# Layer 0's pair gathers: where PE's side work, the spreads of h and two key steps stand between the up products

## The chip, the cores and the metric

The kernel runs on one core of a Trainium2 chip. The metric is the device time of one execution in microseconds (us). Engines are named as in the profile: PE is TensorE (PEld its weight loads), DVE VectorE, ACT ScalarE, POOL GpSimd, SP SyncE.

## What is computed

Two transformer-like blocks in float32 over 256 tokens of width 1024. The first has two layers; each mixes tokens (latent attention, a Fourier branch, a pooling branch, gates) and then runs `_peer`, a lookup of experts. Layer 0 does this for two streams, x and ctx, layer 1's lookup for x alone. The lookup, cut to what matters here:

```
q = (h @ w_pq).reshape(B, L, PEER_HEADS, 2, PEER_QDIM // 2)
s = jnp.einsum("blhpd,hpkd->blhpk", q, peer_keys)
sv, si = lax.top_k(s, PEER_TOPK)                  # 16 of 128 keys, twice per head
...                                               # 16 of the 256 pairs of keys: eidx, gate
a = jnp.einsum("tkd,td->tk", peer_down[eidx], h)  # 8 heads x 16 = 128 experts a token
act = gate * gelu(a)
out = jnp.einsum("tk,tkd->td", act, peer_up[eidx])
```

The second block (feed-forward, convolution, attention over blocks) comes after and is not touched.

## The kernel before, in words

**Gathers.** A row of `peer0` holds an expert's down and up vector, 8 KB. For one stream and one tile of 128 tokens, 128 gathers bring 128 rows each (1 MB). In layer 0 a gather is spread: it brings 4 experts for each of the 32 tokens of one quarter of the tile. There are 4 x 128 = 512 such gathers, in the order x0 tile 0, x0 tile 1, c0 tile 0, c0 tile 1 (x0 and c0 are the two streams in layer 0, x1 and c1 in layer 1). `SPREADS` (line 102) lists for each its index column, its quarter and its set. A set is a group of heads whose routing ends together: heads 0, 1, 2 to 3, 4 to 7 for the first tile and 0 to 3, 4 to 7 for the second. Within a set, all gathers of quarter 0 come first, then those of quarter 1, and so on.

**What one gather n passes through.** POOL issues it (L2825) into one of six places; it waits for up product n-6, that is for its place to be free. DVE multiplies the 128 down vectors with h and sums (`spread_down`, L2347, the "down product", 1.22 us); h lies in PSUM, spread so that each quarter of the partitions holds the 32 tokens of the current quarter. ACT makes the weights in six instructions, the last L1815 (`spread_diag`). PE multiplies them with the up vectors and sums them in PSUM (`spread_up`, L1240, the "up product", four records a gather). Its end lets POOL issue gather n+6. When the quarter changes (`new_quarter`, line 105), PE must spread h anew (`spread_h`, L1227, 16 records), after the last down product of the old quarter and before the first of the new one. There are 48 such spreads.

**Half groups and side work.** `gather` on each engine handles four gathers (`HALF`) and then, or in between, a list of other stages, the side work: query products and scores (`pq`), top-k routing (`route`, on DVE), sending indices to their quarters (`moved`, PE's L1189 and ACT's L1766), gates (`gpre`, `gate`), Fourier steps, attention, output projection, keys and values. `beside_x0` and `beside_c0` say by hand which stages stand in which of the 128 half groups; `scoring` lists those that run before the first gather of a stream, `begin` those of the first half groups.

DVE and ACT do all four down products, or all four weights, and then the side stages. All queues are in order, so weights n+4 stand behind ACT's part of the side stages of half group n, and down product n+4 behind DVE's.

PE does the side stages of half group n first. Inside long products `between()` (called before each matmul, a "piece" below) runs an up product after every fourth piece, up to up n+2. After the stages come what is left of these, then `spread_h(n+4)` if due, then up n+3:

```
last_up[0] = n + HALF - 1
run_stages(stages)
ups_to(n + HALF - 1)
last_up[0] = 0
if n + HALF < len(SPREADS) and new_quarter(n + HALF):
    spread_h(n + HALF)
ups_to(n + HALF)
```

A stage without `between()` (transposes, broadcasts, `moved`) lets no up product through. A query step `pq` has 16 pieces for the queries and 4 for the scores of the block before. SP loads the weight blocks of the side work (`wring`, 1 MB) when the product that used the slot has ended; beside the gathers two slots are in use.

**Places that the change names.** `scoring("x0")` ends with query block 2 and then the routing and sending of the first head; `begin` puts blocks 3 and 4 into half group 0 of x0. `beside_c0` puts layer 1's key steps 0 and 1 (norm of the keys; their transposes) into half group 364, step 2 into 368, step 3 into 372.

Of the kernel before, what the change touches and what calls it, by code (L numbers as in the profile page):

```python
# [13 lines left out]
P = 128  # L14
# [14 lines left out]
TOP = 16  # L29
# [3 lines left out]
HALF = GROUP // 2  # L33
# [20 lines left out]
QUADS = P // QUAD  # L54


def keys_stages(r):
    return [("scale", r, 0), ("norm", r, 0), ("hT", r, 0), ("zA", r, 0), ("zA", r, 1)] + [("kv", r, k) for k in range(4)]
# [8 lines left out]
def branches(r):  # L67

    return [[("zF", r, 0)], [("zF", r, 1)], [("four", r, 0), ("q", r, 0)], [("four", r, 1), ("q", r, 1)], [("q", r, 2)], [("q", r, 3)]]
# [11 lines left out]
def routes(r, t, ks):  # L81

    return [st for k in ks for st in [("route", r, t, k, 0), ("route", r, t, k, 1)] + [("moved", r, t, k)] * (k >= 8 and r != "x1")]


SETS = [[(0, 1), (1, 2), (2, 4), (4, 8)], [(0, 4), (4, 8)]]
# [9 lines left out]

def spread_gathers(t):

    return [(TOP * h0 + QUADS * s + j, j, n) for n, (h0, h1) in enumerate(SETS[t]) for j in range(QUADS) for s in range(TOP * (h1 - h0) // QUADS)]


SPREADS = [g for _ in range(2) for t in range(TT) for g in spread_gathers(t)]


def new_quarter(n):
    return n % P == 0 or SPREADS[n][1:] != SPREADS[n - 1][1:]


def scoring(r):

    first = routes(r, 0, (0, 8))
    return [[("take", r)], [("pq", r, 0)], [("pq", r, 1)], first[0:4], [("pq", r, 2)], first[4:]]


def spread(slots, ranks, counts):

    for n, take in counts:
        while take:
            slots[n].append(ranks[0])
            take -= ranks[0][0] == "route"  # L120
            ranks = ranks[1:]
        if ranks and ranks[0][0] == "moved":
            slots[n + 1].append(ranks[0])
            ranks = ranks[1:]
    assert not ranks


def one_each(n0, count, at):

    where = [at(n0, n) for n in range(count)]  # L130
    return [(n, where.count(n)) for n in sorted(set(where))]


def begin(r, slots):

    slots[0] += [("pq", r, 3)] + [("pq", r, 4)] * (r == "x0") + routes(r, 0, (1,))
    slots[1] += [("pq", r, 5 if r == "x0" else 4)] + routes(r, 0, (9,))[0:2]
    slots[2] += routes(r, 0, (9,))[2:]
    for n, c in ((2, 6), (3, 7), (4, 8)) if r == "x0" else ((3, 5), (5, 6), (7, 7), (9, 8)):
        slots[n].append(("pq", r, c))  # L140
    ranks = routes(r, 0, RANKS[0][4:])
    spread(slots, ranks, ((2, 1), (3, 1), (4, 2), (5, 2), (6, 2), (7, 1), (8, 1), (9, 1), (10, 1), (11, 1), (12, 2), (13, 1)))
# [49 lines left out]
def beside_c0(late):  # L192

    slots = [[] for _ in range(2 * TT * GROUPS)]

    def place(n, st, step=1):
        for i, s in enumerate(st):
            slots[n + i * step].extend(s if isinstance(s, list) else [s])

    at = -1  # L200
    for st in late:
        at += st[0] == "route"
        slots[at + (st[0] == "moved")].append(st)
    at += 1
    spread(slots, routes("c0", 1, RANKS[1]), one_each(at, 20, lambda a, n: a + n - (n + 1) // 5))
    at += 16
    k = keys_stages("x1")
    slots[2].append(k[0])
    slots[4].append(k[1])
    place(5, k[2:5] + [("gpre", "x1", dp, j) for dp in range(3) for j in (1, 2)], 2)  # L210
    assert at < 30
    place(at, [k[5:7]] + k[7:])
    zf0, zf1, one, two, *last = branches("x1")
    place(32, [zf0, [one[1]] + zf1, [one[0]], [two[0]]] + last + [("gpre", "x1", dp, 0) for dp in range(3)], 2)
    slots[39].append(two[1])
    place(50, [("ybc", "x1", 0), ("ybc", "x1", 1), ("gpre", "x1", 3, 1), ("gpre", "x1", 3, 2), ("ybc", "x1", 3), ("ybc", "x1", 2), ("gpre", "x1", 3, 0)], 2)
    slots[40].append(("scale", "c1", 0))
    slots[44].append(("norm", "c1", 0, 0))
    slots[63].append(("hT", "c1", 0, 0))
    return slots  # L220
# [248 lines left out]
def chunk_slots(count):  # L469

    wide, middle, slots, last, used = first_chunks(), middle_chunks(), [], {}, {}
    narrow = narrow_chunks()
    for n in range(count):
        s = n % (SLOTS + ROW_SLOTS) if n < wide else min(range(SLOTS + ROW_SLOTS if n in middle else SLOTS - 1 if n < narrow else SLOTS), key=lambda m: last[m])
        slots.append((s, used.get(s, 0), last.get(s)))
        last[s], used[s] = n, used.get(s, 0) + 1
    return slots


def build(nc, A, out):  # L480
# [19 lines left out]
    with ctx:  # L500
# [46 lines left out]
        at = [0]  # L547
# [155 lines left out]
        slots = chunk_slots(len(plan))  # L703
# [19 lines left out]
        def taken(eng, run, banks):  # L723

            for b in banks:
                eng.wait_ge(bank_free[b], taken_at[run if run == "x1" else "x0", b])
# [6 lines left out]
        def h_mark(run, k, n):  # L733

            firsts = {"c0": 0, "x0": 1, "x1": 4}
            return (firsts[run] if k == 0 else {"x0": 2, "c0": 3, "x1": 5}[run]) * 2 + n
# [19 lines left out]
        def spread_place(n):  # L756

            k = n % SPREAD_PLACES
            return both[k] if k < HALF else lent[n > LENT] if k == HALF else wring[:, SLOTS - 1, :]
# [5 lines left out]
        def _(pe):  # L765
# [42 lines left out]
            next_up, last_up, pieces = [0], [0], [0]  # L808
# [6 lines left out]

            def ups_to(n):
                while next_up[0] < n:
                    spread_up(next_up[0])
                    next_up[0] += 1
                    pieces[0] = 0  # L820
# [393 lines left out]
            def spread_h(n):  # L1214

                run, t = GATHERS[n // P]
                j = SPREADS[n][1]
                pe.wait_ge(mark["h"], h_mark(run, 1, 2))
                if n == 0:
                    taken(pe, run, TAKEN)  # L1220
                else:
                    pe.wait_ge(down_done, n)
                one_of = ident[:, QUAD * j:QUAD * (j + 1)]
                for half in range(2):
                    for i in range(QUADS):
                        qd = QUAD * i
                        ins = pe.matmul(h_ps[qd:qd + QUAD, half * 512:(half + 1) * 512], one_of, h[RUNS[run][0]][:, t, half * 512:(half + 1) * 512],  # L1227
                                        start=True, stop=True, tile_position=(0, qd), skip_group_check=True)
                ins.then_inc(h_spread, 1)

            def spread_up(n):

                t, j = n // P % TT, SPREADS[n][1]
                mine = [k for k in range(n // P * P, n // P * P + P) if SPREADS[k][1] == j]
                if n % P == 0:
                    pe.wait_ge(sum_read, n // P)
                pe.wait_ge(diag_ready, n + 1)
                for half in range(2):
                    qd = QUAD * ((j + 2 * half) % QUADS)
                    ins = pe.matmul(ps[qd:qd + QUAD, UPB + half, :], quad_w[:, n % GROUP, :], spread_place(n)[:, D + half * 512:D + (half + 1) * 512],  # L1240
                                    start=(n == mine[0]), stop=(n == mine[-1]), tile_position=(0, qd), skip_group_check=True)
                ins.then_inc(upp_done, 1)

            def gather(run, t, n0, beside_a, beside_b):

                G = GATHER_NO[run, t]
                for part_, stages in enumerate((beside_a, beside_b)):
                    if run == "x1":
                        i = PAIRS * t + 2 * (2 * n0 + part_)
                        run_stages(stages)  # L1250
                        if i:
                            both_ups(i - 1)
                        both_ups(i)
                        if i == 2 * PAIRS - 2:
                            both_ups(i + 1)
                        continue
                    n = P * G + HALF * (2 * n0 + part_)
                    if n == 0:
                        spread_h(0)
                    last_up[0] = n + HALF - 1  # L1260
                    run_stages(stages)
                    ups_to(n + HALF - 1)
                    last_up[0] = 0
                    if n + HALF < len(SPREADS) and new_quarter(n + HALF):
                        spread_h(n + HALF)
                    ups_to(n + HALF)

            def fb(run, t):
# [1684 lines left out]
```

## Time and profile before

| | us |
|---|---|
| three timed runs | 3846.46, 3848.91, 3853.41 |
| their median | 3848.91 |
| the profiled execution | 3838.83 |
| its span | 3837.0 |
| busy in it: PE, DVE, ACT, POOL | 3174.7, 2396.1, 1605.2, 743.1 |
| DMA traffic | 1158 MB, mean 302 GB/s |

The profiled execution is one run with the hardware profiler; its span goes from its first to its last instruction. All rows below are from it, with times in us from the span's start. Busy times of engines overlap. Layer 0's gathers lie between 367 and 1925 us, layer 1's behind that, then the second block.

### The profile page before, as it was taken

What the parts mean: (1) busy time and instruction counts of PE and PEld (TensorE: products, weight loads), DVE (VectorE), ACT (ScalarE), POOL (GpSimd) and SP (SyncE); (2) the same over time, 40 slices, a digit from 0 to 9 for tenths busy, and PEclk for the clock granted to TensorE, in tenths of its full rate; (3) what the DMA queues carried; (4) which work ended last, traced back from release to release, by engine and by line L of the source; (5) the groups of instructions that cost most, each with busy time, mean ns of one, the idle gap of its engine ahead of it and who ended that gap; (6) DMA issues with size and microseconds to landing.
All of it is one profiled execution on the core that took longest, in us unless ns stands there. A gap on an engine that the chain in (4) does not pass through costs nothing.

```text
span 3837.0 us, 44307 instructions
## 1 busy us (share of the span) xinstructions
PE 3174.7 (83%) x15370; PEld 1938.4 (51%) x15370; DVE 2396.1 (62%) x5191; ACT 1605.2 (42%) x4579; POOL 743.1 (19%) x797
## 2 busy tenths in 40 slices
PE   5898977888896875767778877777799989999899
PEld 2485533233351231122346432333397879898798
DVE  3444678555568777454455887786665866565564
ACT  1432455565555555655542111112233533334433
POOL 0000233233323323333301333333200000000000
PEclk8998998899897887888989989999999989999999
DMA  7665999999999998999925999999754235454454
GB/s 292 271 252 212 343 396 393 356 393 407 409 393 379 388 368 347 407 402 413 418 96 225 396 402 420 401 413 415 295 186 171 93 121 195 165 197 170 142 175 154
DMA packets 163870, 1158.01 MB, mean 302 GB/s; under 512 B 18785, under 2 KB 19553, under 8 KB 26978
## 3 DMA queue, kind: packets, MB, share of 16 engines
q0 software_dynamic: 110592, 805.36, 51.7%
q1 hardware_dynamic: 53090, 350.30, 25.0%
q8 instruction: 99, 1.62, 0.2%
q14 instruction: 89, 0.73, 0.1%
HBM read 1154.53 MB, written 1.05 MB: 301 GB/s over the span
## 4 chain that ended last, share of the span: by engine, by line
PE 54%; DVE 18%; DMA 17%; ACT 6%; issue 4%; POOL 0%; SPq 0%; DVEq 0%; POOLq 0%; ACTq 0%
PE ps L1304 9%; PE ps L1302 9%; PE ps L1303 9%; PE ps L1240 7%; DMA rows<-in_peer,diag 5%; PE ps L1210 4%; DMA h_ctx<-in_peer,idx 3%; PE ps L1159 3%; DMA rows<-in_peer,idx 3%; DMA wring<-in_peer,diag 3%; PE ps L1105 3%; PE ps L903 2%; DVE rows L2347 2%; PE ps L1131 2%; DVE shared L2557 1%
## 5 line engine op out<-in xcount | busy, mean ns | idle before, releaser
L2347 DVE CUSTOM_DVE_ANT_0 rows<-rows,ps 128x1024 f32<-128x1024 f32 x342 | 408.8, 1219 | 304.2 <-DMA rows<-in_peer,diag 228.6
L1240 PE MATMUL ps<-rows,diag 128*32 128x512 f32 x1368 | 413.7, 700 | 178.6 <-ACT diag L1815 175.8
L2825 POOL DMA_INDIRECT rows<-in_peer,diag x342 | 324.2, 948 | 1075.9 <-PE ps L1240 698.1
L1302 PE MATMUL ps<-hT_hi,w_hi 128*128 128x256 f32 x1792 | 508.0, 283 | 8.9 <-DVE hT_lo L2469 8.9
L1304 PE MATMUL ps<-hT_lo,w_hi 128*128 128x256 f32 x1792 | 508.7, 284 | 0.0
L1303 PE MATMUL ps<-hT_hi,w_lo 128*128 128x256 f32 x1792 | 506.9, 283 | 0.0
L1302 PEld LDWEIGHTS ps<-hT_hi,w_hi 128*128 128x128 f32 x1792 | 343.3, 192 | 14.4 <-issue 14.3
L2459 DVE TENSOR_TENSOR w_lo<-wring,w_hi 128x2048 fp32r<-128x2048 f32 x120 | 274.8, 2292 | 112.0 <-ACT w_hi L1874 110.2
L1303 PEld LDWEIGHTS ps<-hT_hi,w_lo 128*128 128x128 f32 x1792 | 342.6, 191 | 0.1
L1304 PEld LDWEIGHTS ps<-hT_lo,w_hi 128*128 128x128 f32 x1792 | 341.5, 191 | 0.0
L1210 PE MATMUL ps<-rows,diag 128*128 128x512 f32 x512 | 252.3, 644 | 80.2 <-ACT diag L1799 73.2
L1806 ACT ACTIVATE g<-a 128x1 f32<-128x1 f32 x512 | 99.7, 195 | 444.4 <-DVE a L2347 443.8
L1240 PEld LDWEIGHTS ps<-rows,diag 128*32 128x32 f32 x1368 | 61.2, 117 | 430.0 <-ACT diag L1815 350.9
L1874 ACT ACTIVATE w_hi<-wring 128x2048 fp32r<-128x2048 f32 x120 | 229.3, 1911 | 112.9 <-DMA wring<-in_wdn 83.6
L1210 PE MATMUL ps<-kvmem,diag 128*128 128x512 f32 x384 | 192.4, 648 | 63.1 <-ACT diag L1799 63.1
L1793 ACT ACTIVATE th<-g 128x2 f32<-128x2 f32 x128 | 26.1, 204 | 488.5 <-DVE g L2326 488.5
L2849 POOL TENSOR_TENSOR ss<-nwt,minus_half 128x1 f32<-128x1 f32 x24 | 13.2, 548 | 1083.4 <-DVE nwt L2031 1083.4
L1210 PEld LDWEIGHTS ps<-rows,diag 128*128 128x128 f32 x512 | 101.2, 205 | 226.1 <-issue 113.6
L1813 ACT ACTIVATE act<-th,gated 128x1 f32<-128x1 f32 x512 | 198.2, 387 | 17.2
L1105 PE MATMUL ps<-hT,wring 128*128 128x256 f32 x768 | 198.6, 403 | 0.1
L2836 POOL DMA_INDIRECT rows<-in_peer,idx x128 | 121.5, 950 | 397.1 <-PE ps L1210 232.4
L2321 DVE CUSTOM_DVE_ANT_0 rows<-rows,ps 128x1024 f32<-128x1024 f32 x128 | 153.7, 1218 | 62.2 <-DMA rows<-in_peer,idx 58.8
(355 smaller groups left out, 6226.2 us busy)
## 6 DMA issues: line engine op xcount, KB each, us to landing
wring<-in_wgu SPq DMA_DIRECT2D x66, 1024.0 KB, 4.9
wring<-in_wdn SPq DMA_DIRECT2D x33, 1024.0 KB, 4.9
wring<-in_wG SPq DMA_DIRECT2D x32, 1024.0 KB, 8.2
wring<-in_wmod SPq DMA_DIRECT2D x28, 1024.0 KB, 7.9
wring<-in_wpq SPq DMA_DIRECT2D x24, 1024.0 KB, 7.2
rows<-in_wgu SPq DMA_DIRECT2D x22, 1024.0 KB, 4.9
rows<-in_wmod SPq DMA_DIRECT2D x20, 1024.0 KB, 7.7
rows<-in_wdn SPq DMA_DIRECT2D x11, 1024.0 KB, 4.8
```

The costliest lines, as they stand in the source:

```text
L1105: last = pe.matmul(b[:, dt * TOK:(dt + 1) * TOK], w[:, k * 256 + dt * P:k * 256 + (dt + 1) * P], hT[:, k, :], start=(k == 0), stop=(k == K ...
L1210: ins = pe.matmul(ps[:, UPB + half, :], diag[:, s, :], both[s][:, D + half * 512:D + (half + 1) * 512], start=(first and j == 0), stop=(la ...
L1240: ins = pe.matmul(ps[qd:qd + QUAD, UPB + half, :], quad_w[:, n % GROUP, :], spread_place(n)[:, D + half * 512:D + (half + 1) * 512], start ...
L1302: pe.matmul(out_, lh[l_at], rh[r_at], start=start, stop=False, skip_group_check=skip)
L1303: pe.matmul(out_, ll[l_at], rh[r_at], start=False, stop=False, skip_group_check=skip)
L1304: return pe.matmul(out_, lh[l_at], rl[r_at], start=False, stop=stop, skip_group_check=skip)
L1813: act.activation(act_, th, ACT.Identity, scale=weight, bias=weight).then_inc(gelu_step, 1)
L1874: act.activation(W2_HI[c % SLOTS2], W2[c % SLOTS2], ACT.Copy).then_inc(hi_ready, 1)
L2321: dve.tensor_tensor_reduce(out=both[c][:, 0:D], in0=both[c][:, 0:D], in1=h_ps, scale=1.0, scalar=0.0, op0=ALU.mult, op1=ALU.add, accum_out ...
L2347: dve.tensor_tensor_reduce(out=down, in0=down, in1=h_ps, scale=1.0, scalar=0.0, op0=ALU.mult, op1=ALU.add, accum_out=a8[:, c:c + 1]).then_ ...
L2459: dve.tensor_tensor(W2_LO[c % SLOTS2], w, W2_HI[c % SLOTS2].bitcast(f32), ALU.subtract).then_inc(lo_ready, 1)
L2825: pool.indirect_dma_start(out=spread_place(n), out_offset=None, in_=A["peer0"], in_offset=bass.IndirectOffsetOnAxis(ap=idx_moved[t][:, col ...
```

## The change

1. The order of quarters in every second set is reversed (0 to 3, then 3 to 0), and `new_quarter` no longer counts a change of set with the same quarter: 40 spreads of h for 48. The eight that fall away are ahead of gathers 16, 32, 64, 192, 272, 288, 320 and 448.
2. In `gather` on PE, up n comes before the side stages of half group n, and `between()` may run all ups up to n+3. `ups_to` itself spreads h for the next half group when it is about to run up n+3.
3. For x0, query block 3 runs before the sending of the first set's indices and so before the first gather; half group 0 keeps block 4.
4. Layer 1's key steps 0, 1, 2 and 3 stand in half groups 364, 368, 372 and 376.

```
 def spread_gathers(t):
-    return [(TOP * h0 + QUADS * s + j, j, n) for n, (h0, h1) in enumerate(SETS[t]) for j in range(QUADS) for s in range(TOP * (h1 - h0) // QUADS)]
+    to_and_fro = range(QUADS), range(QUADS - 1, -1, -1)
+    return [(TOP * h0 + QUADS * s + j, j, n) for n, (h0, h1) in enumerate(SETS[t]) for j in to_and_fro[n % 2] for s in range(TOP * (h1 - h0) // QUADS)]

 def new_quarter(n):
-    return n % P == 0 or SPREADS[n][1:] != SPREADS[n - 1][1:]
+    return n % P == 0 or SPREADS[n][1] != SPREADS[n - 1][1]

 def scoring(r):
     first = routes(r, 0, (0, 8))
-    return [[("take", r)], [("pq", r, 0)], [("pq", r, 1)], first[0:4], [("pq", r, 2)], first[4:]]
+    return [[("take", r)], [("pq", r, 0)], [("pq", r, 1)], first[0:4], [("pq", r, 2)]] + [[("pq", r, 3)], first[4:]] * (r == "x0")

 def begin(r, slots):
-    slots[0] += [("pq", r, 3)] + [("pq", r, 4)] * (r == "x0") + routes(r, 0, (1,))
+    slots[0] += [("pq", r, 4 if r == "x0" else 3)] + routes(r, 0, (1,))

 in beside_c0:
-    place(at, [k[5:7]] + k[7:])
+    place(at, k[5:])

             def ups_to(n):
                 while next_up[0] < n:
+                    k = next_up[0] + 1
+                    if k % HALF == 0 and k < len(SPREADS) and new_quarter(k):
+                        spread_h(k)
                     spread_up(next_up[0])
                     next_up[0] += 1
                     pieces[0] = 0

 in gather on PE:
                     if n == 0:
                         spread_h(0)
-                    last_up[0] = n + HALF - 1
+                    ups_to(n + 1)
+                    last_up[0] = n + HALF
                     run_stages(stages)
-                    ups_to(n + HALF - 1)
                     last_up[0] = 0
-                    if n + HALF < len(SPREADS) and new_quarter(n + HALF):
-                        spread_h(n + HALF)
                     ups_to(n + HALF)
```

## Rows read from the trace of the kernel before

**Rows 1.** The page, DMA engines' busy share in 40 equal slices, in tenths.
```profile
DMA  7665999999999998999925999999754235454454
```
**Rows 2.** Windows: length, busy time (instructions) by engine, PE's clock, DMA share, GB/s.
```profile
367.40:1925.00 1557.60, 1206.87 (x5008) 475.21 (x5006) 963.16 (x2234) 870.98 (x3319) 485.66 (x512) 0.89 0.96 387
...
1505.00:1521.00 16.00, 5.14 (x29) 1.31 (x24) 8.36 (x36) 7.48 (x31) 1.31 (x2) 0.50 0.10 29
```
**Rows 3.** Windows: first query blocks, context's gates and outputs, its queries, half group 216.
```profile
402.80:448.10 45.30, 42.44 (x233) 23.88 (x234) 24.35 (x68) 21.92 (x83) 11.39 (x12) 1.00 0.96 347
892.20:997.60 105.40, 97.60 (x351) 40.86 (x350) 57.64 (x94) 49.87 (x196) 30.62 (x32) 0.98 1.00 409
1035.30:1141.10 105.80, 102.67 (x490) 58.88 (x490) 56.86 (x142) 56.83 (x213) 29.98 (x32) 1.00 1.00 410
1060.42:1072.93 12.51, 12.51 (x57) 7.38 (x56) 4.92 (x8) 7.06 (x28) 4.68 (x5) 1.00 1.01 412
```
**Rows 4.** The page's costliest groups: up products, with PE's idle time before them.
```profile
L1240 PE MATMUL ps<-rows,diag 128*32 128x512 f32 x1368 | 413.7, 700 | 178.6 <-ACT diag L1815 175.8
```
**Rows 5.** Timeline (start, length, engine, line, operation), from half group 216 to 220.
```profile
1069.47 1.05 PE L1170 MATMUL ps<-keysT,shared 128*128 128x128 f32 x8
...
1070.46 1.05 PE L1240 MATMUL ps<-rows,diag 128*32 128x512 f32 x4
...
1070.57 0.60 ACT L1561 ACTIVATE shared<-ps 128x512 f32<-128x512 f32 x1 [0.29 <-PE ps L1170]
...
1071.44 1.56 PE L1159 MATMUL ps<-hT,wring 128*128 128x256 f32 x6
...
1072.40 0.32 ACT L1815 ACTIVATE diag<-quad,act 128x32 f32<-128x32 f32 x1
```
**Rows 6.** Timeline, a gate's last products and the next weights (176 to 180).
```profile
943.74 0.81 PE L1131 MATMUL ps<-ypT,wring 128*128 128x256 f32 x3
...
948.62 0.32 ACT L1815 ACTIVATE diag<-quad,act 128x32 f32<-128x32 f32 x1
```
**Rows 7.** Line L2825 (gathers) from 1035 to 1141: POOL's waits, time to landing.
```profile
  PE ps L1240: 71.5, 30
...
DMA to landing us min/median/max: 5.7/8.5/11.0
```
**Rows 8.** Line L2825 from 892 to 997: time to landing.
```profile
DMA to landing us min/median/max: 6.5/10.6/14.1
```
**Rows 9.** Timeline of PE, layer 1's first transposes and the ups behind them.
```profile
1240.07 3.67 PE L883 MATMUL ps<-ident,h_in 128*128 128x128 f32 x16 [5.99 <-DVE h_in L2123]
1244.71 3.49 PE L1240 MATMUL ps<-rows,diag 128*32 128x512 f32 x8 [0.97 <-ACT diag L1815]
```
**Rows 10.** Line L2347 (down products): DVE's idle time before it until a spread's end.
```profile
  PE ps L1227: 69.7, 17
```
**Rows 11.** Timeline of PE in half group 0 of x0, up to up 4.
```profile
376.43 1.92 PE L1240 MATMUL ps<-rows,diag 128*32 128x512 f32 x4 [8.82 <-ACT diag L1815]
...
389.85 7.07 PE L1159 MATMUL ps<-hT,wring 128*128 128x256 f32 x32
...
397.74 1.92 PE L1227 MATMUL ps<-h_in,ident 128*32 128x512 f32 x16
...
402.82 1.05 PE L1240 MATMUL ps<-x_ctx,diag 128*32 128x512 f32 x4 [0.81 <-ACT diag L1815]
```
**Rows 12.** Timelines of ACT, PE, POOL and DVE at the hole near 1505.
```profile
1507.09 0.32 ACT L1815 ACTIVATE diag<-quad,act 128x32 f32<-128x32 f32 x1
...
1516.13 0.66 PE L939 MATMUL ps<-ident,shared 128*128 128x128 f32 x2 [10.86 <-DVE shared L2148]
1516.71 1.92 PE L1240 MATMUL ps<-kvmem,diag 128*32 128x512 f32 x4
...
1518.92 0.94 POOL L2825 DMA_INDIRECT kvmem<-in_peer,diag  x1 [20.49 <-PE ps L1240]
...
1523.40 1.22 DVE L2347 CUSTOM_DVE_ANT_0 rows<-rows,ps 128x1024 f32<-128x1024 f32 x1 [5.29 <-PE ps L1227]
```
**Rows 13.** Timeline of PE, an up product after a wait.
```profile
1253.94 1.14 PE L1240 MATMUL ps<-kvmem,diag 128*32 128x512 f32 x4 [2.30 <-ACT diag L1815]
```

## The prediction

> **What bounds the kernel now.** I read the page first, for what the DMA engines do in each slice: nine tenths or more in nearly all of slices 5 to 19 (the first is slice 0), and full again in later ones [rows 1]. The change touches layer 0's 512 pair gathers alone. The first is issued at 367.4, the last up product ends at about 1925; over these 1557.6 us the DMA share is 0.96 [rows 2]. So all idle DMA time there is 0.04 x 1557.6 = 62 us, and a change of order can save no more. The longest hole is 1505 to 1521, with a share of 0.10, which is 14.4 us idle [rows 2]. Outside the holes the DMA engines are full, but in places only just. While context's query products run beside the gathers (below: half groups 208 to 236; I name a half group by its first gather) PE is busy 102.67 of 105.8 us at a DMA share of 1.00; for context's gates and outputs (164 to 192) it is 97.60 of 105.4 us, also at 1.00 [rows 3]. There either engine alone can lengthen the stretch. PE's own wait before the up products is for ACT's weights, 175.8 of 178.6 us on the rows buffers [rows 4].
>
> The loop of one half group is what the change rearranges. From up 216 to up 220 it took 12.51 us, PE busy 12.51 of them [rows 3]. Four rows and one weight block of 1 MB (2^20 bytes each) are 5.24 MB, at 412 GB/s [rows 3] 12.7 us. PE and DMA are level.
>
> **Part 1: the first up product ahead of the side work, the last one inside it.** The same instructions are issued. In the old order PE runs three pieces, up n, four, up n+1, four, up n+2, the rest, the spread of h if one is due, up n+3. In the new one: up n, three pieces, up n+1, four, up n+2, four, spread, up n+3, the rest. Then it stands at the wait for up n+4. ACT works in order: its copy of the side product stands ahead of the weights of gather n+4, and can start only when PE's last piece ends. PE's products end at 1069.47 + 1.05 = 1070.52, ACT's copy starts at 1070.57, the weights are there at 1072.40 + 0.32 = 1072.72 [rows 5]: a tail of 2.25 us from last piece to next up. Today up n+3 (1.05) and three pieces (1.56) cover it [rows 5]. Afterwards both stand elsewhere, and nothing covers it.
> - Context's queries, eight half groups. They take 105.8 us [rows 3], which is 8 x 12.5, two spreads of 1.92 and 2 us of waits. After: 8 x (12.5 + 2.25) + 3.8 = 121.8. **+16** (8 if queueing in front of the DMA takes half of it; 20 at most).
> - Context's gates and outputs, eight. Here the tail goes through DVE's mixing, the down product and ACT: a gate's products end at 943.74 + 0.81 = 944.55, the weights are ready at 948.62 + 0.32 = 948.94 [rows 6], 4.4 us. Six of the eight end so (an output's first part is not evacuated). PE's work is 4 ups of 1.0 and products of 7.6, so after: 8 x 11.6 + 1.9 + 6 x 4.4 = 121.1, today 105.4 [rows 3], 16 more. Transfers take 10.6 us from issue to landing here, where the least in the query stretch is 5.7 [rows 7, 8]: up to 4.9 us of lateness may come out of this queueing. **+12** (5 to 17).
> - Attention steps with a gate product (128, 136, 144): a tail of 2.3 or more each, partly absorbed. **+4** (0 to 7).
> - Transposes. The first transposes of context's second norm and of layer 1 (204 and 276) have no places for ups. Today they run in the wait ahead of up n: 3.67 us from 1240.07, then up 276 at 1244.71 and its neighbour right behind [rows 9]. Afterwards they stand between up n and up n+1, so gather n+7 goes out 3.67 later, in a hole, where nothing is queued. **+7** (3 to 7.4).
> - The Fourier and query steps (104 to 120), the norm at 432 and the last transposes at 508 have the same form with more slack: **+5** (0 to 10), by the nearest rows, those of the tail and of the transposes.
> - Gate products in every other half group (from 300 on): the pair needs about 20 us of PE and 22.7 of DMA, so the tail fits: 0.
>
> **Part 2: h spread within the side work, and 40 spreads for 48.** DVE waited 69.7 us in 17 places for a spread [rows 10], 4 each. A spread takes PE 1.92 us [rows 11]. Of the eight that fall away one (row 16) is where PE is the bound; it is counted in part 3. DVE's next down product starts earlier, but its weights stand behind ACT's copy, so this helps only where DVE itself is the bound. Together with up n moved ahead of the index products ("moved") it shortens the other holes, 62 - 14.4 = 48 us in sum, by a little, and later ups pay in some: **-3** (-10 to 0).
>
> **Part 3: x0's query block 3 before the first gather.** The index products of the first set now stand behind 16 + 4 pieces, 7.07 + 1.05 us [rows 5, 11], so the first gather goes out 8.1 later, at 375.5. SP's next weight block goes out when that product ends, about 372 for 389, into an idle DMA; POOL's queue only shifts. In return half group 0 holds 20 pieces for 40. Up 0 at 376.43 + 8.1 = 384.5 [rows 11]; up 1 after 1.9 and four pieces at the lower clock (3.2, estimated as twice today's), up 2 after 2.9, up 3 after 1.0 + 1.9 + 1.9 with the spread, so 397.3; 1.0 + 3.3 to the end of the products, 2.25 of tail: up 4 at 403.9, today 402.82 [rows 11]. Half groups 4 and 8 take 12.5 + 1.9 + 2.25 = 16.65 where they now take 45.3 / 3 = 15.1 [rows 3]; 12, without a spread, 14.75. By row 16 PE is 4 us late, but DVE, which sets the pace from there on and gets its h early, is 1 us early. **+1** (-2 to +4).
>
> **Part 4: layer 1's key steps apart.** Up 364 stands behind the transposes of the normed keys, for which PE waited 10.86 us; its weights were there at 1507.41, it ran at 1516.71, and POOL issued the next gather at 1518.92, after 20.49 us [rows 12]. In the new order up 364 runs at 1507.5 and gather 370 goes out at about 1509, three more by 1514. h for 368 is spread at 1511, so its down product can run when DVE has ended the norm, 1516.1, and not at 1523.40 [rows 12]. What is late next is DVE's routing, which ends at 1504.5, and this norm. Of 14.4 idle us some 5.5 stay: **-9** (-12 to -7).
>
> **Sum.** 16 + 12 + 4 + 7 + 5 - 3 + 1 - 9 = +33 us. The profiled execution took 3838.8 us (span 3837.0), 10 below the median of the timed runs, 3848.9. I add the difference to the median: **3882 us**. Behind 1925 nothing changes; that work waits for the last up product.
>
> **Rivals.**
> - *Queueing swallows the tails* (faster). Place: the joints of half groups 164 to 236. Gathers take 8.5 and 10.6 us to land there, 5.7 at the least [rows 7, 8]. The ups of a group now come early within it; if that keeps rows queued over the tail, only the DMA's 12.7 us per half group count. Then keys (-9), holes (-8) and transposes (+5) are left: -12, 3837. It decides from the point where PE's work and tail fall under 12.7; I get 14.75. Against it: of POOL's waits in the query stretch 71.5 us were for PE [rows 7]. 0.13.
> - *Nothing measurable.* Half of part 1's terms (22) less 12 to 20 from holes and keys: about +2 to +10, taken as 3852. 0.12.
> - *PE's clock falls at the joints* (slower still). After 8.82 us of waiting an up took 1.92 us, at the higher clock 1.05 [rows 11]. The granted clock was 1.00 in the query stretch and 0.50 in the hole at 1505 [rows 2, 3], that is 2.4 and 1.2 GHz. If it fell at half of 20 joints, each would cost 0.87 for the up and 1.5 for three pieces at half the rate: 10 x 2.3 = 23 on top, 3905. 0.12. Against it: after a wait of 2.30 us an up still took 1.14 [rows 13]. The Trainium skill, "TensorE: Matmul & The Clock Gate", section "Loop structure matters more than you think", says that a long wait between bursts lets the clock drop and the next matmul runs cold; by that rule the joints of the gates would be in danger first, and the 1.92 us above agree with it.
>
> **Numbers.** The forecast has 0.63. Faster by over 0.2% (7.7 us, about what a measurement of this kernel can tell from no change) 0.13; within it 0.12; slower 0.63 + 0.12 = 0.75. The bounds of the terms add up to -8 and +58; 3845 to 3908 leaves out the first rival and a little at the top.
>
> **What would show it.** PE's L1240 should wait some 2.3 us for ACT once in each half group from 208 to 236, and up 208 to up 240 should take about 122 us at a DMA share near 0.87. The transposes should follow up 276. The hole near 1505 should shrink to 4 to 6 us and POOL's wait of 20.49 to about 11. The first gather should come at 375.5. I am wrong if the query stretch keeps its 106 us (then the first rival holds), and wrong upwards if ups of 1.92 us fill it.

## The result, and the profile after

The changed kernel takes 3950.42 us (median of 4 runs, 3946.37 to 3958.28), the kernel before 3847.68 beside it: a ratio of 1.0268, 95% interval 1.0246 to 1.029. It is 102.7 us slower. The forecast was 3882, range 3845 to 3908: the sign was right, the size a third of what came. A *joint* below is the place where one half group ends and the next begins, the *tail* the time there from PE's last piece to its next up product.

The page of the changed kernel: PE's granted clock and the DMA engines' share in 40 slices, and the up products' group (busy, mean ns of one, idle time before it).

```profile
PEclk8998998888888888888888999999999989999999
DMA  7766899888888999899962899999955325454444
L1244 PE MATMUL ps<-rows,diag 128*32 128x512 f32 x1368 | 416.7, 703 | 283.1 <-ACT diag L1817 276.0
```

Beside [rows 1], slices 7 to 12 have fallen from nine tenths or more to eight. Beside [rows 4] the same 1368 up products stand behind 283.1 us of idle time, 276.0 of it for ACT's weights, instead of 178.6. The span is 3955.7 us for 3837.0; the profiled execution of the changed kernel is 8 us above its median and that of the kernel before 9 below, so the stretches read here differ by some 16 us more in sum than the medians. The last up product starts at 2039.1 for 1923.8, so 115 of the 119 us more lie ahead of it, in the pair gathers, as the prediction said; behind it little moved.

Windows of the changed kernel from up product to up product (columns as in [rows 2]): up 0 to 20, 20 to 124, 124 to 164 (attention), 164 to 196 (gates, outputs), 208 to 240 (context's queries), 364 to the last.

```profile
381.30:462.20 80.90, 67.28 (x330) 35.77 (x330) 47.44 (x138) 35.70 (x134) 18.87 (x20) 0.94 0.90 338
462.20:797.50 335.30, 251.37 (x1028) 102.40 (x1028) 233.19 (x603) 176.51 (x680) 100.64 (x104) 0.89 0.94 367
797.50:927.00 129.50, 100.33 (x406) 42.23 (x407) 62.97 (x125) 77.38 (x292) 37.56 (x40) 0.87 0.88 345
927.00:1062.90 135.90, 111.35 (x342) 45.14 (x344) 57.88 (x95) 49.70 (x196) 30.10 (x32) 0.87 0.84 323
1101.80:1234.50 132.70, 113.54 (x488) 63.31 (x488) 59.80 (x150) 56.46 (x213) 30.00 (x32) 0.92 0.88 326
1606.90:2039.10 432.20, 313.03 (x1147) 106.24 (x1147) 202.80 (x379) 245.44 (x940) 133.16 (x142) 0.85 0.94 378
```

Three of these between the same ups in the kernel before; the other two are in [rows 3].

```profile
459.40:780.00 320.60, 251.50 (x1050) 98.68 (x1052) 233.00 (x604) 178.11 (x684) 99.57 (x104) 0.90 0.96 383
780.00:892.20 112.20, 92.04 (x408) 38.82 (x407) 62.01 (x123) 75.99 (x289) 37.46 (x40) 0.95 0.98 396
...
1516.70:1923.80 407.10, 307.05 (x1145) 102.24 (x1144) 198.67 (x357) 241.66 (x916) 133.30 (x142) 0.87 0.98 402
```

Read the length minus PE's busy time as PE's idle time, and the two rises apart:

| half groups | before | after | more | PE idle | PE busy |
|---|---|---|---|---|---|
| 20 to 120 | 320.6 | 335.3 | 14.7 | +14.8 | -0.1 |
| 124 to 160 | 112.2 | 129.5 | 17.3 | +9.0 | +8.3 |
| 164 to 192 | 105.4 | 135.9 | 30.5 | +16.8 | +13.8 |
| 208 to 236 | 105.8 | 132.7 | 26.9 | +16.0 | +10.9 |
| 364 to 508 | 407.1 | 432.2 | 25.1 | +19.1 | +6.0 |

The instructions are the same (but for two spreads of h fewer in 20 to 120, and one in 164 to 192 and in 364 to 508; the counts differ by a few more since some records are missing), so a rise of PE's busy time means that it runs slower: the clock column went from 0.95 to 0.87 in attention, from 0.98 to 0.87 in gates and outputs, from 1.00 to 0.92 in the queries. In the queries, the cleanest stretch, PE's idle time rose by the forecast 16 us; the busy part was no term of the sum at all.

One joint of the query stretch in the changed kernel (timeline: start, length, engine, line, operation):

```profile
1144.68 1.05 PE L1174 MATMUL ps<-keysT,shared 128*128 128x128 f32 x8
...
1145.77 0.60 ACT L1563 ACTIVATE shared<-ps 128x512 f32<-128x512 f32 x1 [0.29 <-PE ps L1174]
...
1147.61 0.32 ACT L1817 ACTIVATE diag<-quad,act 128x32 f32<-128x32 f32 x1
...
1147.98 1.05 PE L1244 MATMUL ps<-kvmem,diag 128*32 128x512 f32 x4 [2.25 <-ACT diag L1817]
1148.96 2.68 PE L1163 MATMUL ps<-hT,wring 128*128 128x256 f32 x6
1151.58 1.57 PE L1244 MATMUL ps<-wring,diag 128*32 128x512 f32 x4
1153.08 1.99 PE L1163 MATMUL ps<-hT,wring 128*128 128x256 f32 x8
```

ACT's copy of the last score product, its weights for gather 220, and PE bare for 2.25 us in between: the tail of the prediction, with its length. What follows was not in the prediction's sum. The up product behind the wait still takes 1.05 us, but the next three pieces take 2.68 us where [rows 5] has 1.56, and the next up 1.57; the pieces behind that run as before. At six of the eight joints of the stretch the first up product takes 1.05 us like this one, at 224 and 228 it takes 1.83 and 1.35, behind waits of 2.25 and 2.35 us. PE's waits in that stretch and in gates and outputs, and the up product behind one of the gates:

```profile
PE ps L1244 <- ACT diag L1817: 18.3, 8, 2.5
```
```profile
PE ps L1244 <- ACT diag L1817: 26.0, 7, 4.5
```
```profile
962.38 1.92 PE L1244 MATMUL ps<-kvmem,diag 128*32 128x512 f32 x4 [4.45 <-ACT diag L1817]
```

Here, behind 4.45 us, the up itself runs at the lower rate.

The other parts. The hole of part 4, with the transposes now behind the up (PE, then POOL):

```profile
1606.95 1.07 PE L1244 MATMUL ps<-kvmem,diag 128*32 128x512 f32 x2 [10.79 <-ACT diag L1817]
...
1609.15 0.94 POOL L2827 DMA_INDIRECT kvmem<-in_peer,diag  x1 [11.22 <-PE ps L1244]
```

POOL waits 11.22 us where [rows 12] has 20.49 (forecast about 11). The up stands 10.79 us itself, now for its own weights behind DVE's norm. The hole in the transfers has shrunk as forecast: 15 x 0.34 = 5.1 us idle for 14.4.

```profile
1597.00:1612.00 15.00, 5.05 (x40) 2.22 (x42) 11.27 (x19) 6.32 (x26) 2.80 (x3) 0.66 0.66 261
```

Layer 1's first transposes follow up 276, as forecast:

```profile
1337.22 1.92 PE L1244 MATMUL ps<-rows,diag 128*32 128x512 f32 x4 [8.78 <-ACT diag L1817]
1339.07 2.59 PE L887 MATMUL ps<-ident,h_in 128*128 128x128 f32 x16
```

The first gather is issued at 372.11, 4.7 us later than before, not 8.1.

### The profile page after: what moved, and what is told of

Same layout as the page of the kernel before. It is cut to its first block, busy times and chain, and to the rows that moved or that the text cites. A ratio compares the mean times of both kernels' runs of the same rounds, so it can differ in the third digit from the quotient of the medians.

```text
span 3955.7 us, 44041 instructions
## 1 busy us (share of the span) xinstructions
PE 3202.7 (81%) x15242; PEld 1952.5 (49%) x15242; DVE 2394.6 (61%) x5191; ACT 1600.9 (40%) x4579; POOL 742.7 (19%) x797
## 3 DMA queue, kind: packets, MB, share of 16 engines
HBM read 1154.53 MB, written 1.05 MB: 292 GB/s over the span
## 4 chain that ended last, share of the span: by engine, by line
PE 57%; DVE 16%; DMA 15%; ACT 8%; issue 3%; POOL 0%; SPq 0%; DVEq 0%; ACTq 0%; POOLq 0%
PE ps L1304 9%; PE ps L1306 9%; PE ps L1305 9%; PE ps L1244 8%; PE ps L1214 4%; DMA rows<-in_peer,diag 4%; PE ps L1163 4%; PE ps L1109 4%; DMA h_ctx<-in_peer,idx 3%; DMA rows<-in_peer,idx 3%; PE ps L907 2%; PE ps L1135 2%; DVE rows L2349 2%; DMA kvmem<-in_peer,diag 2%; ACT act L1815 1%
## 5 line engine op out<-in xcount | busy, mean ns | idle before, releaser
L1244 PE MATMUL ps<-rows,diag 128*32 128x512 f32 x1368 | 416.7, 703 | 283.1 <-ACT diag L1817 276.0
L2349 DVE CUSTOM_DVE_ANT_0 rows<-rows,ps 128x1024 f32<-128x1024 f32 x342 | 408.6, 1219 | 359.7 <-DMA rows<-in_peer,diag 278.1
L1304 PEld LDWEIGHTS ps<-hT_hi,w_hi 128*128 128x128 f32 x1792 | 343.9, 192 | 14.4 <-issue 14.3
L1244 PEld LDWEIGHTS ps<-rows,diag 128*32 128x32 f32 x1368 | 60.3, 117 | 532.5 <-ACT diag L1817 437.0
L1109 PEld LDWEIGHTS ps<-hT,wring 128*128 128x128 f32 x768 | 145.8, 200 | 99.9 <-issue 82.4
```

Of the source, the lines that this page charges most:

```text
L1109: last = pe.matmul(b[:, dt * TOK:(dt + 1) * TOK], w[:, k * 256 + dt * P:k * 256 + (dt + 1) * P], hT[:, k, :], start=(k == 0), stop=(k == K ...
L1304: pe.matmul(out_, lh[l_at], rh[r_at], start=start, stop=False, skip_group_check=skip)
L2349: dve.tensor_tensor_reduce(out=down, in0=down, in1=h_ps, scale=1.0, scalar=0.0, op0=ALU.mult, op1=ALU.add, accum_out=a8[:, c:c + 1]).then_ ...
```

## The experiments

In what follows a stretch is named by its ups. The parts are numbered as in the prediction: *part 1* is the order on PE (first up product ahead, last one inside), *part 2* the order of the quarters. The spread of h inside the side work, which the prediction counts to part 2, comes and goes with part 1 in every run.

**The changed kernel without part 1.**

```
-                    k = next_up[0] + 1
-                    if k % HALF == 0 and k < len(SPREADS) and new_quarter(k):
-                        spread_h(k)
 in gather on PE: the lines of before
```

> The changed kernel with PE's loop of before for a half group (side work, the last up product behind it, h spread at the end): parts 2, 3 and 4 stay, part 1 is gone. Theory A (the whole loss is the joint of two half groups, where PE stands before the first up product: 184.5 us before, 366.1 us after): 3848 - 9 (keys) - 3 (quarters) + 1 (query block) = 3837, within 3828 to 3846. Theory B (a good part of the loss comes from the later first gather, the quarters to and fro or the key steps): over 3860.

Measured: 3839.61 us, ratio 0.9972 (0.9961 to 0.9983): faster than the kernel before. Its query stretch:

```profile
1038.40:1144.20 105.80, 102.67 (x490) 58.74 (x492) 56.92 (x142) 56.83 (x213) 29.98 (x32) 1.00 1.01 410
```

It is that of [rows 3] to the hundredth in PE's busy time. So part 1 (with its spreads of h) costs 3950.4 - 3839.6 = 111 us, and parts 2 to 4 together give about 9. Theory B falls.

**Which half of part 1?** First the last up product, and the spread of h in front of it, put behind the side work again:

```
-                    last_up[0] = n + HALF
+                    last_up[0] = n + HALF - 1
```

> The changed kernel, but the last up product of a half group, and the spread of h in front of it, stand behind the side work again; the first stays ahead. Theory A: the last piece's tail (piece, ACT's copy, ACT's weights) is then covered by 1.05 us of up product, and by 1.92 more where h is spread; at some 45 joints with side work that is 45 x 1.05 + 15 x 1 = 62 off, 3888 (3870 to 3910). Theory B (the harm is in the first up product ahead, not in the bare tail): 3940 or more. Theory C (the harm is the last up product inside the side work): 3855 or less.

Measured: 3916.33, ratio 1.017 (1.015 to 1.0191). 34 of the 111 us come back, less than theory A's 62 and 6 us outside its range; theories B and C do not fit either. In the query stretch theory A holds:

```profile
1078.10:1193.60 115.50, 102.10 (x490) 59.84 (x492) 56.80 (x142) 56.87 (x213) 29.97 (x32) 1.00 0.97 373
```

With the up product of 1.05 us over the tail, 8 x (2.25 - 1.05) = 9.6 on top of 105.8 are due, and 9.7 show. The clock is 1.00 again: most joints of this stretch now wait 1.27 us, and PE's busy time is back at 102.10. Elsewhere cover of one up was worth less than I had summed; why is not shown.

**Side work ahead again, the last up product still inside.**

```
-                    ups_to(n + 1)
                     last_up[0] = n + HALF
```

> The changed kernel, but the side work begins ahead of the first up product again, as before; the last up product and the spread of h stay within the side work. Theory A: at the joint the next half group's first three pieces (1.56 us with query products) cover the tail of 2.25 us but for 0.7, so the context's queries (half groups 208 to 236) lose 8 x 0.7 = 6 us at most and the whole stands at 3837 + 6 = 3843 (3832 to 3860). Theory C (last up product inside the side work does the harm, since nothing stands behind the last piece): 3900 or more.

Measured: 3894.52, ratio 1.0123 (1.0106 to 1.014). That is far outside theory A's range and near theory C, and the query stretch even took what the changed kernel's does. Its window, and the joint near 1106 on PE's timeline:

```profile
1062.20:1195.60 133.40, 113.50 (x482) 63.91 (x483) 59.89 (x148) 56.66 (x213) 29.98 (x32) 0.91 0.88 328
```
```profile
1105.13 1.05 PE L1174 MATMUL ps<-keysT,shared 128*128 128x128 f32 x8
1108.52 1.05 PE L1244 MATMUL ps<-kvmem,diag 128*32 128x512 f32 x4 [2.34 <-ACT diag L1816]
```

No piece stands between the last score product and the first up. `between()` counts pieces since the last up product. Where that one is inside, the pieces behind it are counted into the next half group; with four score products behind it, the next up is due at once. The edit had not put the side work first where it mattered.

**The same with the count cleared.**

```
-                    ups_to(n + 1)
+                    pieces[0] = 0
                     last_up[0] = n + HALF
```

> The changed kernel with the side work ahead of the first up product and the last one within it, as the run before, but with the count of pieces set to 0 at the start of each half group. Theory A': in that run the count was carried over from the pieces behind the last up product (four score products in the context's query steps), so the first up product was due at once and stood bare at the joint although the code put the side work ahead; its query stretch took 133.4 us, as the changed kernel's 132.7. With the count at 0, three pieces of 0.39 us or more lead and cover all but 0.7 of the 2.25: the query stretch takes 106 to 112 us and the whole 3840 to 3860. Theory C (a last up product inside the side work is bad by itself): the query stretch stays near 133 and the whole at 3890 or more.

Measured: 3864.52, ratio 1.0039 (1.0027 to 1.0051), 4.5 us above the expected band. The query stretch:

```profile
1054.70:1167.30 112.60, 103.41 (x490) 57.88 (x492) 58.58 (x146) 56.64 (x212) 30.03 (x32) 1.00 0.98 385
```
```profile
PE ps L1244 <- ACT diag L1817: 8.9, 9, 1.6
```

Three pieces cover the tail but for 0.95 us at most joints, and 133.4 us become 112.6, at the upper end of what A' has; C falls. The rest above the kernel before lies there (7 us), in attention (7) and in the gates (up 164 to 180 takes 68.2 us, 57.8 before), where the tail of 4.4 us is longer than three pieces.

**The clock by itself.** PE is kept busy at the joints from 124 to 240 by products of zero weights (8 a joint, 16 behind gates and outputs), which leave the accumulator as it is. The added product, without the loop around it:

```
+                        pe.matmul(ps[qd:qd + QUAD, UPB, 0:P], ident[0:QUAD, QUAD:2 * QUAD], ident[0:QUAD, :],
+                              start=False, stop=False, tile_position=(0, qd), skip_group_check=True)
                     ups_to(n + 1)
```

> The changed kernel with PE kept busy while it waits at the joints of half groups 124 to 240: 8 products of zero weights (32 x 32 by 128 columns, 16 behind gates and outputs) added into the up product's own accumulator, which they leave as it is. They lie in a wait of 2.25 us or more. Theory A with the clock (after a wait PE's products run at the lower clock: PE's busy time in those stretches rose by 8.3, 4.7, 9.0 and 10.9 us): up to 33 us come back, 3917 to 3935. Theory D (the lower clock costs nothing, since the wait for rows sets the pace): 3945 to 3955. If the products outlast the wait, they push the time up, past 3955.

Measured: 3950.3, ratio 1.0269 (1.0249 to 1.0289): nothing gained in sum, as theory D has it. By stretch it is two things, up 180 to 196 (16 products a joint) and the queries (8):

```profile
999.90:1068.70 68.80, 68.80 (x260) 28.85 (x260) 24.64 (x41) 25.67 (x101) 15.12 (x16) 0.90 0.77 284
1106.50:1229.40 122.90, 118.62 (x616) 71.95 (x616) 60.05 (x150) 56.47 (x212) 29.99 (x32) 1.00 0.93 353
```

The first was 60.9 us in the changed kernel and now has no idle time at all: at two of its four joints (184 and 192) there was no wait to fill, at the others 3.38 us, and the filling takes 3.7 at each. The second fell by 9.8, at a clock of 1.00. So it was tried with the query stretch alone.

> The changed kernel with PE kept busy in the wait at the joints 212 to 240 alone, by 8 products of zero weights each. In the run that did it from 124 to 240 the query stretch fell from 132.7 to 122.9 us at a granted clock of 1.00 for 0.92, but 16 products per joint outlasted the waits behind the outputs (60.9 to 68.8 us), so the whole stood still. Theory A with the clock: 8 joints x 1.36 = 10.9, of which 9.8 show: 3940 (3935 to 3945). Theory D (no gain from the clock; the 9.8 were a shift between stretches): 3950.

Measured: 3944.24, ratio 1.024 (1.0225 to 1.0255). The query stretch, and its groups on PE (busy, mean ns of one, idle before); behind it the pieces of the same stretch in the changed kernel:

```profile
1102.60:1227.10 124.50, 120.20 (x616) 72.50 (x616) 60.08 (x150) 56.48 (x213) 29.98 (x32) 0.99 0.93 348
```
```profile
L1163 PE MATMUL ps<-hT,wring 128*128 128x256 f32 x256 | 64.5, 395 | 0.0
...
L1252 PE MATMUL ps<-ident 32*32 32x128 f32 x128 | 15.4, 269 | 0.0
```
```profile
L1163 PE MATMUL ps<-hT,wring 128*128 128x256 f32 x256 | 70.8, 424 | 0.0
```

The stretch became 8.2 us shorter, and the pieces alone take 6.3 us less. The filling is 15.4 / 8 = 1.9 us a joint, inside the 2.25. The median of the whole fell by 6.2, within the range, but the intervals of the two kernels touch (1.0225 to 1.0255, 1.0246 to 1.029), so the whole by itself doesn't show it. The stretch does, in two runs: work added in a wait made it shorter, so the clock is a cost of its own here, and about a microsecond a joint of it came back.

**Is it the queue on ACT and DVE?** PE's order stays the changed one; the next half group's first down product and weights go ahead of the side work on DVE and ACT, where no new spread is due (so 128 keeps the old order too, beside the six that the expectation lists).

```
+def early(n):
+    return int(124 < n < 244 and not new_quarter(n))

 in gather on ACT and on DVE:
-                        for k in range(n, n + HALF):
+                        for k in range(n + early(n), n + HALF + early(n + HALF)):
```

> The changed kernel; DVE's down product and ACT's weights of the next half group's first gather stand ahead of this half group's side work on their engines, from half group 124 to 240, wherever that gather needs no new spread of h (22 of 29 joints; 144, 160, 176, 208, 224 and 240 keep the old order). PE's order is untouched. Theory A (the bare tail, and it is one of queue order: ACT's copy or DVE's mixing in front of the weights): the freed joints lose tail and lower clock, 6 x (2.25 + 1.4) = 22 in the query stretch (132.7 to 111), 26 of 30 in gates and outputs, 12 of 17 in attention: 3890 (3880 to 3910). Rival (the rows themselves come too late, the joint waits for the transfer whatever stands in ACT's queue): the shifted down product holds up the side work behind it, 3935 or more.

Measured: 3889.51, ratio 1.0104 (1.0085 to 1.0123); gates with outputs and queries:

```profile
914.70:1023.90 109.20, 99.71 (x341) 42.00 (x342) 55.35 (x91) 50.12 (x195) 30.46 (x33) 0.95 0.96 384
1063.60:1175.70 112.10, 106.60 (x490) 60.30 (x491) 60.26 (x150) 56.98 (x213) 30.05 (x32) 0.97 0.98 384
```

111 was expected in the queries and 112.1 came; gates and outputs gave back 26.7 (26 expected), attention 9.8 (12). At a freed joint the weights are ready before PE ends its pieces, and the up follows them with no gap:

```profile
1097.01 0.32 ACT L1821 ACTIVATE diag<-quad,act 128x32 f32<-128x32 f32 x1
...
1101.90 1.05 PE L1178 MATMUL ps<-keysT,shared 128*128 128x128 f32 x8
...
1102.89 1.05 PE L1248 MATMUL ps<-kvmem,diag 128*32 128x512 f32 x4
```

The rows were there in time, so the rival falls: the wait was made by what stood ahead of the weights in two queues.

**Where the rest lies.** The old order on PE between half groups 124 and 240 only.

```
+                    old = 124 <= n < 244
+                    if not old:
+                        ups_to(n + 1)
+                    last_up[0] = n + HALF - old
```

> The changed kernel, but PE keeps its order of before in half groups 124 to 240 (attention, gates, outputs, norm, context's queries); part 1 stands everywhere else. Up 124 to up 240 took 355.2 us in the kernel before, 361.9 with the old order throughout (without part 1), 438.0 in the changed kernel. Theory A (losses add up by joint): the 76 us of this stretch go, the other 35 stay: 3840 + 35 = 3875 (3865 to 3885). Rival 1 (the prediction's: elsewhere transfers or DVE set the pace and part 1 is nearly free): 3840 to 3850. Rival 2 (the stretches hang together, lateness being absorbed further on): 3890 or more.

(From up 124 to up 240 the profiles have 361.1 us before, 361.9 without part 1 and 437.0 changed, so the expectation's 355.2 and 438.0 are wrong, and the loss in the stretch is 75 us for its 76.)

Measured: 3878.29, ratio 1.0092 (1.0077 to 1.0107); the stretch takes

```profile
796.80:1160.30 363.50, 317.49 (x1320) 144.02 (x1320) 199.42 (x402) 206.68 (x779) 109.51 (x116) 0.94 0.99 402
```

Against the changed kernel, 72 us go and 3878.3 - 3839.6 = 39 stay, for 35 expected. Both rivals fall: the losses add up by stretch, and outside the middle part 1 is far from free. Side by side with the kernel without part 1 (both have 40 spreads of h):

| ups | without part 1 | this kernel | more | PE idle | PE busy |
|---|---|---|---|---|---|
| 0 to 20 | 69.5 | 80.9 | 11.4 | +10.0 | +1.4 |
| 20 to 124 | 328.5 | 332.3 | 3.8 | -2.1 | +5.9 |
| 240 to 364 | 364.7 | 370.8 | 6.1 | +9.0 | -2.9 |
| 364 to the last | 411.3 | 424.6 | 13.3 | +15.7 | -2.4 |

These are single executions with a few records missing in each, so a row is good to some us; in sum 33 of the 35 us are idle time of PE and 2 are busy time. Outside the middle part 1 costs waits and hardly any clock. PE's waits there for weights, from up 364 on, in this kernel and in the kernel before:

```profile
PE ps L1244 <- ACT diag L1819: 113.4, 61, 10.9
```
```profile
PE ps L1240 <- ACT diag L1815: 88.4, 68, 7.7
```

10.9 of the first is the wait at part 4's hole, which is no loss; 14 remain.

**The other parts alone**, each on the kernel before.

Part 4:

> The kernel before with part 4 alone (layer 1's last key steps apart). Theory A: the hole near 1505 shrinks from 14.4 to some 5 us idle, as in the run with the old order, where up 300 to up 364 took 194.6 us for 204.2: 9 off, 3839 (3836 to 3843). Rival: the gain is eaten by 436, since the steps moved apart push the later ones: 3845 or more.

Measured: 3840.0 for 3850.28 beside it, ratio 0.9974 (0.9965 to 0.9984). POOL's wait at the hole:

```profile
1514.36 0.94 POOL L2825 DMA_INDIRECT kvmem<-in_peer,diag  x1 [11.23 <-PE ps L1240]
```

Part 3:

> The kernel before with part 3 alone (x0's query block 3 ahead of the first gather). By the prediction +1: 3849 (3846 to 3852). By the run with the old order, which stood 5.7 us ahead at up 20 but 2.2 behind at up 124: the early lead is lost again at a wait that does not depend on it, 3846 to 3850. Rival: the lead lasts, 3842.

Measured: 3848.95 for 3850.28, ratio 0.9996 (0.9984 to 1.0007): no difference.

Part 2, quarters to and fro with 40 spreads, each still behind the side work:

> The kernel before with the quarters to and fro alone (40 spreads of h for 48). Theory A: 3 off, 3845 (3838 to 3848): each spread saved gives 1.92 us of PE where PE bounds and up to 4 of DVE's waiting where DVE does. Rival: the spreads saved lie where the transfers set the pace, 3848.

Measured: 3846.12 for 3850.28, ratio 0.9991 (0.9982 to 0.9999): some 4 us, just clear of no difference. Up 8 to 20 takes 36.5 us for 41.5.

Parts 2 and 4 together:

> The kernel before with parts 2 (quarters to and fro) and 4 (key steps apart), without parts 1 and 3. The two alone gave 4 and 10 us. Theory A (they act at different places, 8 to 20 and 364, and add up): 3836 (3832 to 3840), the best so far. Rival (what the first wins is lost again at 100 to 124 and at 384 to 436, as in the run with the old order, which stood at 3840): 3840.

Measured: 3843.72 for 3848.64, ratio 0.9979 (0.9969 to 0.999). They did not add up measurably; neither expected figure was met (the rival's 3840 is nearer), and the intervals of this run, of part 4 alone and of parts 2 to 4 overlap. All three are faster than both kernels, by about a quarter of a per cent against the kernel before; part 4 alone is the smallest edit that does it.

## Why the prediction was right and wrong

**Right.** What bounds the kernel; the mechanism and its place. The tail at the joints was forecast at 2.25 us in the queries and 4.4 in the gates; the profile has 2.25 and 4.45. PE's L1244 waits once per half group in the query stretch, eight times, 18.3 us. Moving the weights ahead took the wait away without touching PE. Part 4 was put at -9 and measured -10. For the other two the match says less. Part 2 was put at -3 and measured -4, but the run had only the quarters and not the spread inside the side work; part 3 was put at +1 within the new order of part 1 and measured -1 in the old one. The DMA share of the query stretch, 0.88 for 0.87, is luck: the 0.87 was 105.8 / 121.8, and for the measured 132.7 us the same division gives 0.80, which is what the moved bytes did (326 GB/s for 410).

**Wrong: part 1's sum, 44 us against 111.** Of the 67 us that were missing, the clock accounts for 33, waits in attention for 5, the credit for queueing for 5 and what lies outside the middle for 27 (39 where 5 + 7 stood). These add up to 70, near enough for figures from single executions. Three steps of the sum failed.

- *The lower clock was a rival, not a term.* The prediction held it apart "on top" with a chance of 0.12, as a case of its own at 3905, and let [rows 13] speak against it: an up product of 1.14 us behind a wait of 2.30. That row looks at the wrong instruction. The next up product of the same kernel before ran at the lower rate:

```profile
1255.50 1.92 PE L1240 MATMUL ps<-wring,diag 128*32 128x512 f32 x4 [0.42 <-ACT diag L1815]
```

Here too the up behind the wait keeps its 1.05 at most joints of the queries; it is the pieces behind it that slow down, 2.68 for 1.56 (and behind 4.45 us the up as well). The sign that the prediction named for being wrong upwards, ups of 1.92 us, would have missed it. From 124 to 160, 164 to 192 and 208 to 236 PE's busy time rose by 8.3 + 13.8 + 10.9 = 33 us. The rival's 2.3 us for a joint was too high (10.9 / 8 = 1.4 in the queries), its ten joints too few. The Trainium skill ("TensorE: Matmul & The Clock Gate", section "Loop structure matters more than you think") has the next matmul run cold after a long wait. The 1.92 us behind 4.45 agree with it; behind 2.25 us the first up product mostly did not, and the pieces after it did.
- *Queueing was credited.* Gates and outputs stood at 16 and were cut to 12, since 4.9 us of queueing before the rows landed might swallow a part. PE's idle time rose by 16.8. The median landing fell from 10.6 us [rows 8] to the one below, and from 8.5 [rows 7] to 6.8 in the queries: my reading, which no run isolates, is that such slack is used up once and not at every joint, and that PE is late from then on.

```profile
DMA to landing us min/median/max: 5.2/7.1/10.2
```

- *Joints that I had not priced.* Attention was +4, for the three half groups with a gate product, and measured +17.3, of which 9.0 is idle time: its other joints wait too (4.91 us ahead of up 132, 3.74 ahead of 140 and 148). "Gate products in every other half group: 0" and "+5" for Fourier steps, norm and last transposes cover the ground outside 124 to 240, where 39 us were measured. The argument for 0, that the pair of half groups has time over, compared sums of PE's work with sums of transfers; the DMA share from up 364 on fell from 0.98 to 0.94 all the same, with 19.1 us more of PE's idle time. For 0 to 20, folded into part 3, half group 4 was put at 16.65 us and took 18.9. For the pair of half groups the prediction's own rate of 412 GB/s gives 22.9 us of transfers, not 22.7, which changes nothing.

The transposes (+7 forecast, bounds 3 to 7.4) cannot be read apart: up 196 to 208 rose by 1.3 and 276 to 300 by 2.2, together at the low end. No run isolated them.

**The rivals.** That queueing swallows the tails is refuted by the query stretch: 132.7 us for 105.8, at a DMA share of 0.88 for 1.00. "Nothing measurable" is too. The clock rival named the missing cost but as a branch; added as a term with the measured 33 us it would have put the forecast at 3915, still short by the joints left out.

## What to carry to other kernels

Before moving an engine's work across a joint, ask what the next instruction there waits for and what stands ahead of *that* in the other engines' queues: PE's last piece was followed at once by the up product whose weights were queued behind that very piece's evacuation, 2.25 us at each joint of the queries, 4.45 at those of the gates. Price every joint, the ones with "time over" as well, and be slow to take credit for a queue. And a forecast cost that comes together with the mechanism (here the clock behind each wait) belongs into the sum, not among the rivals.

## What the runs showed of the hardware

- The lower clock can show late behind a short wait: at the joint shown, after 2.25 us, the up took its 1.05, the six records behind it 2.68 / 6 = 0.45 us each for 0.26, and 5 us after the wait all ran at full rate again. At six of that stretch's eight joints the first up ran at full rate, at two it did not. With waits of 0.95 or 1.27 us at most joints of the same stretch the granted clock stayed at 1.00.
- Products that compute nothing, 1.9 us of them in each wait of 2.25, made the query stretch shorter: 124.5 and 122.9 us in two runs, for 132.7, at a granted clock of 0.99 and 1.00 for 0.92.
